# Attention queries and keys turned by VectorE squares and a round trip through device memory, in a two-layer hybrid decoder kernel

## The chip, the cores and the metric

The kernel runs on one core of a Trainium2 chip. The metric is the device time of one execution in microseconds (us). The kernel before takes 824.13 us, the median of three runs (824.0 to 824.54). One more execution was profiled; all rows of the trace come from it.

## What is computed (the reference, cut)

Two decoder layers on x of 256 tokens by 2048 columns, float32. Each layer reads four groups of heads off one projection h @ w_in (6232 columns), gates them, joins them and adds the product with w_out (2048 by 2048) to x.

```python
h = rmsnorm(x)
u = h @ w_in
y = concat(GLA(...) * silu(g_a), SSD(..., g_b), MLA(...) * silu(g_c), DIL(...) * silu(g_d))
x = x + y @ w_out

# MLA: 4 heads, q and k of 128 plain + 64 rotated columns, causal, 256 keys
q, k = rmsnorm(q) * q_head_g, rmsnorm(k) * k_head_g
q, k = rope on the last 64 columns
o = softmax(mask(q @ k.T * 192 ** -0.5)) @ v

# DIL: 4 heads of 128 columns, three dilated windows, rope on all columns
o = softmax(taps(q @ k.T * 128 ** -0.5)) @ v
```

To form q @ k.T on TensorE, queries and keys must lie with the 128 columns of a head on the partitions and the tokens along the row. They are produced the other way round, with tokens on the partitions. So each layer turns four matrices of 256 tokens by 512 columns: the plain parts of the MLA queries and keys, and the DIL queries and keys. That turning is what the change is about. The rotated MLA parts (a fifth such step, "mla rT") are turned as before.

## The kernel before, in words

**The weight stream.** Both layers are one long stream of weight units. A unit is two row blocks of 128 by up to 512 columns (512 KB for a unit of 1024 columns per partition, 278 KB in the narrow blocks). A layer has 144 numbered units n, 8 to a block of columns, and 4 extra ones for the MLA projections (STREAM, line 103), 148 in all. For each unit SP loads it into one of 4 buffers `raw` (line 495), ScalarE rounds it to `w_hi` (line 997), VectorE forms the rest `w_lo` (line 1354), and TensorE does 8 products with w_hi (lines 665 and 666) and then 4 with w_lo (line 674). w_hi and w_lo have 4 buffers each. So SP loads unit n only when VectorE has made w_lo of unit n - 4 (line 490), and ScalarE rounds unit n only when TensorE is through with unit n - 4 (line 996). In the text "lo 103" is the w_lo of unit 103, and "hi 95" the w_hi of unit 95.

**The side work.** All that is not this stream is cut into named steps, written between the units on each engine: after unit n of TensorE (PE_AT, line 186), after hi n on ScalarE (lines 1203 to 1297) and after lo n on VectorE (lines 1647 to 1768). Each engine works strictly in this order, so a step that waits holds up the hi or lo behind it. The dictionary ORDER (line 227) writes down the resulting order of the named steps; a step signals by a counter of its engine, and others wait for that count.

**The steps around the change**, in the numbers of the units they stand behind (TensorE / ScalarE / VectorE):

- VectorE 77 to 82 normalises the MLA heads, 83 and 84 do their rope, 86 and 87 normalise the DIL heads, 88 to 91 do their rope (lines 1578 to 1598).
- "mla qT", "mla kT", "mla rT" (lines 888 to 897, heads_T line 841): TensorE 85, 86, 87 turns 8 tiles of 128 by 128 each into PSUM, line 846; ScalarE copies them to SBUF behind 88, 89, 90 (line 1187).
- "dil qT", "dil kT" (lines 914 to 918): the same, TensorE 95 and 97, ScalarE 98 and 100.
- Scores "S 0" and "S 1" (line 849), two heads each: MLA at TensorE 89 and 93, DIL at 99 and 103. VectorE adds the mask and takes the row maximum three units later (smax, lines 1608 to 1616: 92, 96, 102, 106), ScalarE takes the exponential (line 1195, same units). For DIL, VectorE then multiplies by the tap counts (lines 1620 to 1626).
- "PT" turns the probabilities on TensorE (line 872; MLA 92 and 96, DIL 102 and 106), ScalarE copies them (line 1201; MLA 95 and 99). "O" multiplies by the values (lines 883 to 885; 94, 98, 104, 108), and VectorE scales the result (line 1644; 97, 101, 107, 111).
- The finished first and second groups are turned by VectorE itself, 16 transposes of 32 by 256 each (y_turn, line 1368; turn, line 1317), behind 97 to 100 and 101 to 104, into the first 1024 columns of u.
- ScalarE evacuates the gate blocks from PSUM (evac, line 1017) behind 90, 98, 106 and 114, with two table loads each (lines 1033 and 1036).

TensorE's side steps use two PSUM banks in turn; the step after next waits for the last reader of a bank (LAST_READER, line 196).

Of the kernel before, what the change touches and what calls it, by code (L numbers as in the profile page):

```python
# [27 lines left out]
ACT = mybir.ActivationFunctionType  # L28
# [158 lines left out]
for _n in range(8):  # L187
# [3 lines left out]
          "mla kv 1": KV_AT, "ssd Y": 76, "ssd yb": 81, "mla qT": 85, "mla kT": 86, "mla rT": 87, "mla S 0": 89, "mla PT 0": 92,  # L191
          "mla S 1": 93, "mla O 0": 94, "dil qT": 95, "mla PT 1": 96, "dil kT": 97, "mla O 1": 98, "dil S 0": 99,
# [7 lines left out]
               "mla cT": ("dve", "mla cT"), "mla qT": ("act", "mla qT"), "mla kT": ("act", "mla kT"), "mla rT": ("act", "mla rT"),  # L200
               "dil qT": ("act", "dil qT"), "dil kT": ("act", "dil kT")}
LAST_READER |= {f"gla level {n}": ("dve", f"gla merge {n}") for n in range(1, 8)}
LAST_READER |= {f"mla {w} {t}": ("act", f"mla {w} {t}") for w in ("q", "kv") for t in range(2)}
for _m in ("mla", "dil"):
    for _i in range(2):
# [25 lines left out]
        "mla cT, ssd Y, ssd yb, mla qT, mla kT, mla rT, "  # L231
        "mla S 0, mla PT 0, mla S 1, mla O 0, dil qT, mla PT 1, dil kT, mla O 1, dil S 0, dil PT 0, dil S 1, dil O 0, "
# [7 lines left out]
        "mla rT, mla P 0, ssd rs sum, mla PT 0, mla P 1, evac 11, dil qT, mla PT 1, dil kT, dil P 0, dil PT 0, "  # L240
# [7 lines left out]
        "mla n 0 0, mla n 0 1, ssd yT, mla n 1 0, mla n 1 1, mla rope products, mla rope, dil n 0 0, dil n 0 1, "  # L248
        "dil n 1 0, dil n 1 1, dil rope 0 products, dil rope 0, dil rope 1 products, dil rope 1, mla max 0, "
# [10 lines left out]
def build(nc, xT_d, x_d, pos_d, cols_d, w_d, params_d, gla_w2, gla_b,  # L260
          consts_d, masks_d, out_d):
    ctx = ExitStack()
    with ctx:
# [39 lines left out]
        eps, minus_half, log_scale = powers[:, 0:8], powers[:, 8:16], powers[:, 16:17]  # L303

# [65 lines left out]
        yturned = [u[:, t, 0:1024].rearrange("p (k s) -> p k s", k=4) for t in range(2)]  # L370
# [57 lines left out]
        warm = sem("warm")  # L428
        setup_chain = sem("setup_chain")
# [53 lines left out]
        @block.sync  # L483
        def _(sp):

            xT_load(sp, 0)
            sp.dma_start(raw[:, 0, 0:WB], weights(0, 0)[:, 0:WB]).then_inc(first_in, 16)
            for l in range(DEPTH):
                for g, n in enumerate(STREAM):
                    sp.wait_ge(split_done, l * PER_LAYER + g + 1)  # L490
                    if (l, n) == (0, 0):

                        sp.dma_start(raw[:, 0, WB:2 * WB], weights(l, n)[:, WB:2 * WB]).then_inc(weights_in[0], 16)
                    else:
                        sp.dma_start(raw[:, g % RAW, 0:unit_columns(n)], weights(l, n)).then_inc(weights_in[g % RAW], 16)
                    if (l, n) == (0, 0):
                        xT_load(sp, 1)
                    if l == 0 and n < len(XT_PARTS) - 2:
                        xT_load(sp, n + 2)
                    if (l, n) == (0, CONSTS_LOAD):  # L500
                        sp.dma_start(cst[:, 0:C_FR], consts_d[:, 0:C_FR]).then_inc(consts_in, 16)
                        sp.dma_start(lmask[:, :, :].rearrange("p a b -> p (a b)"), masks_d).then_inc(consts_in, 16)
                    if n in ROWS_LOAD:

                        i = ROWS_LOAD.index(n)
                        sp.wait_ge(row_out, 16 * (l + 1))
                        sp.dma_start(rows[:, 2 * i:2 * i + 2, :], row_d[2 * i:2 * i + 2, :].partition_broadcast(P)).then_inc(row_in[i], 16)
                    if n == PARAMS_LOAD[l]:
                        if l:

                            sp.wait_ge(*reached("dve", l - 1)(f"y {GB}"))
                        sp.dma_start(param_rows[:, :], params_d[l]).then_inc(params_in, 16)
                    if l == 0 and n in X_LOAD:
                        i = X_LOAD.index(n)
                        t, c = i // 2, slice(i % 2 * D // 2, (i % 2 + 1) * D // 2)
                        sp.dma_start(x[:, t, c], x_d.rearrange("o (t p) n -> p (o t) n", p=P)[:, t, c]).then_inc(x_in[i], 16)

            for i in range(len(OUT_PARTS)):
# [75 lines left out]
        def _(pe):  # L594
# [15 lines left out]
            for l in range(DEPTH):  # L610
# [277 lines left out]
                def mla_qT():  # L888
                    pe.wait_ge(*dve("mla rope"))
                    heads_T("mla qT", lambda t, h: mqk[:, t, h, 0:P])  # L890

                def mla_kT():
                    heads_T("mla kT", lambda t, h: mqk[:, t, 4 + h, 0:P])

                def mla_rT():
                    rr = mrr.rearrange("p t (a b) d -> p t a (b d)", b=2)
                    heads_T("mla rT", lambda t, h: rr[:, t, h])
# [3 lines left out]
                       "mla qT": mla_qT, "mla kT": mla_kT, "mla rT": mla_rT}  # L901

                def stages(n):
                    for name in PE_AT:
# [9 lines left out]
                        elif name == "dil qT":  # L914
                            pe.wait_ge(*dve("dil rope 1"))
                            heads_T(name, lambda t, h: dqk[:, t, h])
                        elif name == "dil kT":
                            heads_T(name, lambda t, h: dqk[:, t, 4 + h])
# [38 lines left out]
        def _(act_):  # L957
# [23 lines left out]
            for l in range(DEPTH):  # L981
# [202 lines left out]

                def heads_T(name, dst):
                    act_.wait_ge(*pe(name))
                    A_(dst, pair_of(name).rearrange("p b (k s) -> p (b k) s", k=2), ACT.Copy).then_inc(*signal("act", name))  # L1187
# [15 lines left out]
                for place, n in enumerate(STREAM):  # L1203
# [74 lines left out]
                    if n == slot("mla qT"):  # L1278
                        heads_T("mla qT", mqT)
                    if n == slot("mla kT"):  # L1280
                        heads_T("mla kT", mkT)
                    if n == slot("mla rT"):
                        heads_T("mla rT", mrT.rearrange("p a b s -> p (a b) s"))
                    if n == slot("dil qT"):
                        heads_T("dil qT", dqT)
                    if n == slot("dil kT"):
                        heads_T("dil kT", dkT)
# [14 lines left out]
        def _(v):  # L1302
# [29 lines left out]
            for l in range(DEPTH):  # L1332
# [314 lines left out]
                for place, n in enumerate(STREAM):  # L1647
# [157 lines left out]
```

## Time and profile before

| | us |
|---|---|
| median of 3 runs | 824.13 (824.0 to 824.54) |
| the profiled execution | 823.59 |
| its span, first to last instruction | 821.6 |
| TensorE busy in the span | 816.4 |
| VectorE busy | 625.2 |
| ScalarE busy | 478.2 |
| granted TensorE clock | 1.0 of full speed throughout |

The span is 2 us less than the execution's own time. Busy time is what the hardware recorded for each engine; idle time before an instruction is put down to what released it.

### The profile page before, as it was taken

The numbers are of one execution on the slowest core, as the hardware profiler recorded it, in microseconds if no ns is written. First come the engines' busy times: TensorE is split into PE (matmuls) and PEld (weight loads), VectorE is DVE, ScalarE is ACT, GpSimd is POOL, SyncE is SP. The second block draws the span as 40 slices with busy tenths as digits, with TensorE's granted clock in tenths as the row PEclk, the third lists the DMA queues.
The fourth block names the chain that finished last, engine by engine and source line by source line (L and its number), as shares of the span: only waits on it lengthen the run. The fifth ranks groups of instructions, "written<-read, shape, count | busy, mean of one in ns | idle before, by whom it ended". The sixth has DMA issues, their size and how long they took to land.

```text
span 821.6 us, 11397 instructions
## 1 busy us (share of the span) xinstructions
PE 816.4 (99%) x4244; PEld 693.0 (84%) x4244; DVE 625.2 (76%) x1118; ACT 478.2 (58%) x788; POOL 54.1 (7%) x64
## 2 busy tenths in 40 slices
PE   9999999999999999999999999999999999999998
PEld 5888888999888888888888888889998888888886
DVE  6678799876886986678965977979769868965542
ACT  6665534777865566433556464357697665654341
POOL 7200000200200000000000000002012000000000
PEclk9999999999999999999999999999999999999999
DMA  9956634566654445655576655457657433456653
GB/s 333 352 204 211 192 129 153 145 208 180 208 176 154 129 132 201 191 191 187 177 253 184 200 161 169 129 147 200 191 173 220 164 129 129 158 177 210 196 189 119
DMA packets 47607, 150.98 MB, mean 184 GB/s; under 512 B 5504, under 2 KB 6192, under 8 KB 47552
## 3 DMA queue, kind: packets, MB, share of 16 engines
q1 hardware_dynamic: 47040, 149.98, 57.0%
q8 instruction: 33, 0.54, 0.3%
q10 hardware_dynamic: 320, 0.21, 0.1%
q14 instruction: 22, 0.18, 0.1%
q0 software_dynamic: 192, 0.07, 0.1%
HBM read 148.13 MB, written 2.11 MB: 183 GB/s over the span
## 4 chain that ended last, share of the span: by engine, by line
PE 91%; DVE 7%; issue 2%; DMA 1%; SPq 0%; ACT 0%; DVEq 0%
PE gemm L665 26%; PE gemm L674 26%; PE gemm L666 26%; DVE arena L1323 3%; DVE w_lo L1354 2%; PE pairs L857 1%; PE pairs L846 1%; PE pairs L833 1%; PE pairs L838 1%; PE pairs L834 1%; PE pairs L795 1%; PE pairs L731 1%; DVE arena L1433 1%; PE pairs L872 1%; DMA u<-in_xT_dram 1%
## 5 line engine op out<-in xcount | busy, mean ns | idle before, releaser
L1354 DVE TENSOR_TENSOR w_lo<-raw,w_hi 128x1024 fp32r<-128x1024 f32 (+2 forms) x295 | 324.7, 1110 | 144.4 <-ACT w_hi L997 142.9
L665 PE MATMUL gemm<-w_hi,a_hi 128*128 128x512 f32 (+1 forms) x1144 | 421.6, 374 | 0.0
L666 PE MATMUL gemm<-w_hi,a_lo 128*128 128x512 f32 (+1 forms) x1144 | 414.4, 368 | 0.0
L997 ACT ACTIVATE w_hi<-raw 128x1024 fp32r<-128x1024 f32 (+2 forms) x295 | 281.0, 967 | 191.4 <-PE gemm L674 136.1
L674 PE MATMUL gemm<-w_lo,a_hi 128*128 128x512 f32 (+1 forms) x1144 | 281.8, 368 | 0.3
L665 PEld LDWEIGHTS gemm<-w_hi,a_hi 128*128 128x128 f32 x1144 | 215.2, 188 | 35.6 <-issue 1.3
L666 PEld LDWEIGHTS gemm<-w_hi,a_lo 128*128 128x128 f32 x1144 | 215.3, 188 | 33.0
L674 PEld LDWEIGHTS gemm<-w_lo,a_hi 128*128 128x128 f32 x1144 | 203.2, 188 | 36.6 <-DVE w_lo L1354 2.0
L573 POOL TENSOR_TENSOR st<-st,powers 128x4 f32<-128x4 f32 (+2 forms) x8 | 8.6, 1074 | 431.5 <-ACT arena L1075 213.4
L1195 ACT ACTIVATE arena<-arena,st 128x128 f32<-128x128 f32 (+1 forms) x32 | 13.1, 444 | 35.4 <-DVE st L1616 35.4
L1027 ACT ACTIVATE u<-gemm,st 128x512 f32<-128x512 f32 (+1 forms) x40 | 22.1, 605 | 18.8 <-PE gemm L674 18.8
L1323 DVE STREAM_TRANSPOSE arena<-u 32x256 f32<-32x256 f32 x64 | 27.9, 436 | 1.2
L1323 DVE STREAM_TRANSPOSE u<-o 32x256 f32<-32x256 f32 x64 | 27.9, 435 | 1.0
L1323 DVE STREAM_TRANSPOSE u<-x 32x256 f32<-32x256 f32 x48 | 20.9, 436 | 0.6
L1182 ACT ACTIVATE arena<-u 128x192 f32<-128x192 f32 (+1 forms) x64 | 20.6, 330 | 0.8 <-PE pairs L795 0.8
L1514 DVE SCALAR_TENSOR_TENSOR u<-arena,allp,u 128x256 f32<-128x256 f32 x48 | 20.9, 474 | 0.0
L1583 DVE SCALAR_TENSOR_TENSOR u<-u,sth,param_rows 128x192 f32<-128x192 f32 (+1 forms) x64 | 19.9, 378 | 0.0
L1058 ACT ACTIVATE arena<-arena 128x256 f32<-128x256 f32 x16 | 6.8, 424 | 18.0 <-DVE arena L1405 18.0
L1187 ACT ACTIVATE arena<-pairs 128x1024 f32<-128x1024 f32 x10 | 10.3, 1027 | 11.7 <-PE pairs L846 11.7
L731 PEld LDWEIGHTS pairs<-arena 128*128 128x128 f32 x112 | 14.7, 191 | 1.2
L1473 DVE COPY_PREDICATED o<-lmask,pairs 128x512 f32<-128x512 uint8 x14 | 12.4, 888 | 4.2 <-issue 4.2
L1314 DVE SCALAR_TENSOR_TENSOR a_lo<-u,allp,a_hi 128x256 fp32r<-128x256 f32 x28 | 14.3, 558 | 1.6 <-ACT a_hi L978 1.5
(200 smaller groups left out, 639.0 us busy)
## 6 DMA issues: line engine op xcount, KB each, us to landing
raw<-in_weights_dram SPq DMA_DIRECT2D x225, 512.0 KB, 4.1
raw<-in_weights_dram SPq DMA_DIRECT2D x64, 278.0 KB, 3.1
raw<-in_weights_dram SPq DMA_DIRECT2D x6, 384.0 KB, 3.4
x<-in_x_dram SPq DMA_DIRECT2D x4, 512.0 KB, 6.2
o<-ssd_rows SPq DMA_DIRECT2D x8, 256.0 KB, 4.9
param_rows<-in_params_dram SPq DMA_DIRECT2D x2, 904.0 KB, 7.1
u<-in_xT_dram SPq DMA_DIRECT2D x3, 512.0 KB, 8.1
out_dram<-x SPq DMA_DIRECT2D x3, 512.0 KB, 6.4
```

The lines of the kernel that those rows point to most:

```text
L665: pe.matmul(acc_t[t], a_hi[:, k, tok[t]], hi, start=k == 0, stop=False)
L666: pe.matmul(acc_t[t], a_lo[:, k, tok[t]], hi, start=False, stop=False)
L674: last = pe.matmul(acc_ps[:, b % 2, t, 0:w], a_hi[:, k, t * P:(t + 1) * P], lo, start=False, stop=k == KT - 1)
L731: last = pe.matmul(to, W[:, p, t * P:(t + 1) * P], Ql[n % 2][:, :, t, p, :], start=True, stop=True)
L997: A_(w_hi[:, g % SPLIT, 0:c], raw[:, g % RAW, 0:c], ACT.Copy).then_inc(hi_done, 1)
L1027: last = A_(u[:, t, c0 - N_GATE:c0 - N_GATE + w], acc_ps[:, b % 2, t, 0:w], ACT.Copy, scale=xrs[:, t:t + 1])
L1182: last = A_(sq[j % 8] if m == "mla" else sq[:, t, h, :], buf[:, t, 4 * i + h, :], ACT.Square, scale=buf.shape[-1] ** -0.5, accum_out=total ...
L1314: last = v.scalar_tensor_tensor(a_lo[:, k, :], part, gain(l, k), a_hi[:, k, :].bitcast(F32), ALU.mult, ALU.subtract)
L1323: last = v.transpose(to[32 * f:32 * f + 32, :, :, i, :], rows[32 * i:32 * i + 32, :, :, f, :])
L1354: TT(w_lo[:, g % SPLIT, 0:c], raw[:, g % RAW, 0:c], w_hi[:, g % SPLIT, 0:c].bitcast(F32), ALU.subtract).then_inc(split_done, 1)
L1514: last = STT(conv(f), xc[:, f, j:j + S], tap_weight(l, j, f), conv(f), ALU.mult, ALU.add)
L1583: last = STT(buf[:, t, 4 * i + h, :], buf[:, t, 4 * i + h, :], rs[:, j:j + 1], g, ALU.mult, ALU.mult)
```

## The change: what it does

The four turnings leave TensorE. Each becomes three steps.

1. VectorE transposes the 32 by 32 squares in place (turn_squares): two instructions of 128 partitions by 512 elements, one for each half of the tokens. They stand behind lo 79 (MLA queries), 83 (MLA keys), 90 (DIL queries) and 92 (DIL keys). The result goes to a new buffer `fold` or to columns 6656 to 7679 of the arena.
2. SP stores the 512 KB into device memory in one transfer, at unit at + 5, where `at` is the number above.
3. SP waits at unit at + 7 until that has landed, and loads it back in four transfers, one for each 32 partitions: 128 KB each, in pieces of 1 KB.

ScalarE then copies the result into the tiles that the scores read, behind hi 86, 88, 95 and 97 (before: 88, 89, 98, 100), from SBUF instead of PSUM. It waits for the four transfers of that name there. VectorE gets three new waits: the squares of the DIL queries and keys wait until the stores of the MLA ones have landed, and so does the first DIL rope (its scratch overlaps the MLA keys' squares). The turned y goes to the arena instead of u, and waits for "mla S 1" instead of "mla rT". SP's queue is the one that also loads the weights.

```diff
@@ PE_AT, LAST_READER and ORDER["pe"] @@
-          "mla kv 1": KV_AT, "ssd Y": 76, "ssd yb": 81, "mla qT": 85, "mla kT": 86, "mla rT": 87, "mla S 0": 89, "mla PT 0": 92,
-          "mla S 1": 93, "mla O 0": 94, "dil qT": 95, "mla PT 1": 96, "dil kT": 97, "mla O 1": 98, "dil S 0": 99,
+          "mla kv 1": KV_AT, "ssd Y": 76, "ssd yb": 81, "mla rT": 87, "mla S 0": 89, "mla PT 0": 92,
+          "mla S 1": 93, "mla O 0": 94, "mla PT 1": 96, "mla O 1": 98, "dil S 0": 99,
...
@@ ORDER["act"] @@
-        "mla rT, mla P 0, ssd rs sum, mla PT 0, mla P 1, evac 11, dil qT, mla PT 1, dil kT, dil P 0, dil PT 0, "
+        "mla rT, mla P 0, ssd rs sum, dil qT, mla PT 0, mla P 1, dil kT, evac 11, mla PT 1, dil P 0, dil PT 0, "
@@ ORDER["dve"] @@
-        "mla n 0 0, mla n 0 1, ssd yT, mla n 1 0, mla n 1 1, mla rope products, mla rope, dil n 0 0, dil n 0 1, "
-        "dil n 1 0, dil n 1 1, dil rope 0 products, dil rope 0, dil rope 1 products, dil rope 1, mla max 0, "
+        "mla n 0 0, mla n 0 1, ssd yT, mla q squares, mla n 1 0, mla n 1 1, mla k squares, mla rope products, mla rope, dil n 0 0, dil n 0 1, "
+        "dil n 1 0, dil n 1 1, dil rope 0 products, dil rope 0, dil q squares, dil rope 1 products, dil rope 1, dil k squares, mla max 0, "
@@ build @@
+        fold = sb("fold", [P, S * 4])
...
-        yturned = [u[:, t, 0:1024].rearrange("p (k s) -> p k s", k=4) for t in range(2)]
+        SQUARES = {}
+        SQUARES["mla q"] = fold[:, :], A(3072, 1024), 79
+        SQUARES["mla k"] = A(6656, 1024), u[:, 1, 0:1024], 83
+        SQUARES["dil q"] = fold[:, :], u[:, 0, 0:1024], 90
+        SQUARES["dil k"] = A(6656, 1024), u[:, 1, 0:1024], 92
+
+        HEADS_AT = {"mla q": 86, "mla k": 88, "dil q": 95, "dil k": 97}
+
+        yturned = [A(t * 1024, 1024, "p (k s) -> p k s", k=4) for t in range(2)]
...
+        squares_d = {name: nc.dram_tensor(name.replace(" ", "_") + "_squares", (P, 4 * S), F32, kind="Internal").ap() for name in SQUARES}
@@ SP @@
+            def squares_out(l, name):
+
+                sp.wait_ge(*reached("dve", l)(f"{name} squares"))
+                sp.dma_start(squares_d[name], SQUARES[name][0]).then_inc(squares_out_done[name], 16)
+
+            def squares_back(l, name):
+
+                sp.wait_ge(squares_out_done[name], 16 * (l + 1))
+                away, to = squares_d[name].rearrange("(i b) (f c) -> f b i c", b=32, f=4), SQUARES[name][1]
+                for f in range(4):
+                    sp.dma_start(to[32 * f:32 * f + 32].rearrange("b (i c) -> b i c", i=4), away[f]).then_inc(squares_in[name], 16)
...
+                    for name, (_, _, at) in SQUARES.items():
+                        if n == at + 5:
+                            squares_out(l, name)
+                        if n == at + 7:
+                            squares_back(l, name)
@@ TensorE @@
-                def mla_qT():
-                    pe.wait_ge(*dve("mla rope"))
-                    heads_T("mla qT", lambda t, h: mqk[:, t, h, 0:P])
-
-                def mla_kT():
-                    heads_T("mla kT", lambda t, h: mqk[:, t, 4 + h, 0:P])
-
                 def mla_rT():
+                    pe.wait_ge(*dve("mla rope"))
...
-                        elif name == "dil qT":
-                            pe.wait_ge(*dve("dil rope 1"))
-                            heads_T(name, lambda t, h: dqk[:, t, h])
-                        elif name == "dil kT":
-                            heads_T(name, lambda t, h: dqk[:, t, 4 + h])
@@ ScalarE @@
                 def heads_T(name, dst):
-                    act_.wait_ge(*pe(name))
-                    A_(dst, pair_of(name).rearrange("p b (k s) -> p (b k) s", k=2), ACT.Copy).then_inc(*signal("act", name))
+
+                    act_.wait_ge(squares_in[name], 16 * 4 * (l + 1))
+                    act_.wait_ge(*dve("mla rope" if name[:3] == "mla" else "dil rope 1"))
+                    A_(dst.rearrange("p h (t i a) -> p i (h t) a", t=T, i=4), SQUARES[name][1].rearrange("p (i c a) -> p i c a", i=4, a=32), ACT.Copy).then_inc(*signal("act", name + "T"))
...
+                    for name, to in (("mla q", mqT), ("mla k", mkT), ("dil q", dqT), ("dil k", dkT)):
+                        if n == HEADS_AT[name]:
+                            heads_T(name, to)
@@ VectorE @@
+            def turn_squares(to, rows):
+
+
+                to = to.rearrange("p (f k t a) -> p t k f a", f=4, k=4, t=T)
+                for t in range(T):
+                    last = v.transpose(to[:, t], rows[:, t].rearrange("p k (f b) -> p k f b", f=4))
+                return last
...
-                    v.wait_ge(*pe("mla rT"))
+
+                    v.wait_ge(*pe("mla S 1"))
...
+                def head_squares(name):
+
+                    m, i = name[:3], "qk".index(name[4])
+
+                    if m == "dil":
+                        v.wait_ge(squares_out_done["mla " + name[4]], 16 * (l + 1))
+                    elif l:
+                        v.wait_ge(squares_out_done["dil " + name[4]], 16 * l)
+                    v.wait_ge(*me(f"mla n {i} 1" if m == "mla" else f"dil rope {i}"))
+                    heads = (mqk if m == "mla" else dqk)[:, :, 4 * i:4 * i + 4, 0:P]
+                    turn_squares(SQUARES[name][0], heads).then_inc(*sig(f"{name} squares"))
...
                 def rope_products(name, after, x1, x2, tmp, nh, hd, step):
                     v.wait_ge(setup["act"], 1)
+                    if name == "dil rope 0":
+                        v.wait_ge(squares_out_done["mla k"], 16 * (l + 1))
...
+                    for name in HEADS_AT:
+                        if n == SQUARES[name][2]:
+                            head_squares(name)
```

## Rows read from the trace of the kernel before

**Rows 1.** The page, part 1: busy time, share of the span, instructions.
```profile
PE 816.4 (99%) x4244; PEld 693.0 (84%) x4244; DVE 625.2 (76%) x1118; ACT 478.2 (58%) x788; POOL 54.1 (7%) x64
```

**Rows 2.** The page, part 4: the chain that ended last, by engine.
```profile
PE 91%; DVE 7%; issue 2%; DMA 1%; SPq 0%; ACT 0%; DVEq 0%
```

**Rows 3.** The chain, first layer, then unit 103 of both: start, us, what.
```profile
232.63 0.87 PE pairs L846 x8
236.25 0.87 PE pairs L846 x8
...
242.60 0.91 PE gemm L674 x4
245.32 0.92 PE gemm L674 x4
...
296.26 0.92 PE gemm L674 x4
...
702.08 0.92 PE gemm L674 x4
```

**Rows 4.** Timeline of TensorE: PT of the first DIL heads, third part of unit 103.
```profile
293.61 0.82 PE L872 MATMUL pairs<-cst,arena 128*128 128x128 f32 x6
...
296.10 1.08 PE L674 MATMUL gemm<-w_lo,a_hi 128*128 128x512 f32 x4
```

**Rows 5.** Groups of instructions, shapes apart: count, busy us, mean ns, idle before.
```profile
L1323 DVE STREAM_TRANSPOSE u<-o 32x256 f32<-32x256 f32 x64 | 27.9, 435 | 1.0
L1419 DVE TENSOR_TENSOR arena<-o,arena 128x256 f32<-128x256 f32 x16 | 6.7, 420 | 0.6 <-ACT arena L1060 0.6
L1590 DVE TENSOR_TENSOR arena<-u,sincos 128x512 f32<-128x512 f32 x6 | 4.1, 684 | 0.0
L1187 ACT ACTIVATE arena<-pairs 128x1024 f32<-128x1024 f32 x10 | 10.3, 1027 | 11.7 <-PE pairs L846 11.7
```

**Rows 6.** Timeline of VectorE: lo 91, first and last of smax 0, lo 93, lo 97, y turn, lo 103.
```profile
245.03 1.22 DVE L1354 TENSOR_TENSOR w_lo<-raw,w_hi 128x1024 fp32r<-128x1024 f32 x1 [2.23 <-ACT w_hi L997]
...
248.52 0.29 DVE L1612 CUSTOM_DVE_ANT_0 arena<-pairs,cst 128x128 f32<-128x128 f32 x1
...
249.75 0.17 DVE L1616 TENSOR_SCALAR st<-st 128x4 f32<-128x4 f32 x1
252.80 1.23 DVE L1354 TENSOR_TENSOR w_lo<-raw,w_hi 128x1024 fp32r<-128x1024 f32 x1 [2.88 <-ACT w_hi L997]
...
266.74 1.22 DVE L1354 TENSOR_TENSOR w_lo<-raw,w_hi 128x1024 fp32r<-128x1024 f32 x1 [1.30 <-ACT w_hi L997]
...
290.92 1.78 DVE L1323 STREAM_TRANSPOSE u<-o 32x256 f32<-32x256 f32 x4
292.71 1.23 DVE L1354 TENSOR_TENSOR w_lo<-raw,w_hi 128x1024 fp32r<-128x1024 f32 x1
```

**Rows 7.** Timeline of VectorE, second layer: lo 103.
```profile
698.54 1.23 DVE L1354 TENSOR_TENSOR w_lo<-raw,w_hi 128x1024 fp32r<-128x1024 f32 x1
```

**Rows 8.** Timeline of ScalarE: hi 95, mla PT 0, hi 96, hi 97.
```profile
256.82 1.04 ACT L997 ACTIVATE w_hi<-raw 128x1024 fp32r<-128x1024 f32 x1
257.77 0.79 ACT L1201 ACTIVATE arena<-pairs 128x768 f32<-128x768 f32 x1
258.46 1.04 ACT L997 ACTIVATE w_hi<-raw 128x1024 fp32r<-128x1024 f32 x1
...
265.67 1.99 ACT L997 ACTIVATE w_hi<-raw 128x1024 fp32r<-128x1024 f32 x2
```

**Rows 9.** Transfers: issues, KB each, median us to landing; the first from 205 to 300 us.
```profile
raw<-in_weights_dram SPq DMA_DIRECT2D x28, 512.0 KB, 3.5
...
x<-in_x_dram SPq DMA_DIRECT2D x4, 512.0 KB, 6.2
o<-ssd_rows SPq DMA_DIRECT2D x8, 256.0 KB, 4.9
...
out_dram<-x SPq DMA_DIRECT2D x3, 512.0 KB, 6.4
```

More of the change, by code:

```diff
@@ L199 @@
                "ssd cum": ("dve", "ssd row"), "ssd gcol": ("act", "ssd gcol"), "ssd CB": ("dve", "ssd CB"), "ssd Y": ("dve", "ssd yT"), "ssd yb": ("act", "ssd y"),
-               "mla cT": ("dve", "mla cT"), "mla qT": ("act", "mla qT"), "mla kT": ("act", "mla kT"), "mla rT": ("act", "mla rT"),
-               "dil qT": ("act", "dil qT"), "dil kT": ("act", "dil kT")}
+               "mla cT": ("dve", "mla cT"), "mla rT": ("act", "mla rT")}
 LAST_READER |= {f"gla level {n}": ("dve", f"gla merge {n}") for n in range(1, 8)}
@@ L230 @@
         "gla level 6, gla level 7, gla out, ssd cum, ssd gcol, ssd CB, ssd xs, "
-        "mla cT, ssd Y, ssd yb, mla qT, mla kT, mla rT, "
-        "mla S 0, mla PT 0, mla S 1, mla O 0, dil qT, mla PT 1, dil kT, mla O 1, dil S 0, dil PT 0, dil S 1, dil O 0, "
+        "mla cT, ssd Y, ssd yb, mla rT, "
+        "mla S 0, mla PT 0, mla S 1, mla O 0, mla PT 1, mla O 1, dil S 0, dil PT 0, dil S 1, dil O 0, "
         "dil PT 1, dil O 1, yT 2, yT 3",
@@ L428, in build @@
         warm = sem("warm")
+        squares_out_done, squares_in = ({name: sem(name.replace(" ", "_") + end) for name in SQUARES} for end in ("_squares_out", "_squares_in"))
+        squares_d = {name: nc.dram_tensor(name.replace(" ", "_") + "_squares", (P, 4 * S), F32, kind="Internal").ap() for name in SQUARES}
         setup_chain = sem("setup_chain")
@@ L886, in values, with mla_rT @@
                     last.then_inc(*signal("pe", f"{m} O {i}"))
-                def mla_qT():
+                def mla_rT():
                     pe.wait_ge(*dve("mla rope"))
-                    heads_T("mla qT", lambda t, h: mqk[:, t, h, 0:P])
-                def mla_kT():
-                    heads_T("mla kT", lambda t, h: mqk[:, t, 4 + h, 0:P])
-                def mla_rT():
                     rr = mrr.rearrange("p t (a b) d -> p t a (b d)", b=2)
@@ L900, in _ @@
                        "gla out": gla_out, "ssd xs": ssd_xs, "ssd cum": ssd_cum, "ssd gcol": ssd_gcol, "ssd CB": ssd_CB, "ssd Y": ssd_Y, "ssd yb": ssd_yb, "mla cT": mla_cT,
-                       "mla qT": mla_qT, "mla kT": mla_kT, "mla rT": mla_rT}
+                       "mla rT": mla_rT}
                 def stages(n):
@@ L1183, in head_sums, with mla_rT @@
                     last.then_inc(*signal("act", f"{m} rs {i} sum"))
+                def mla_rT():
+                    act_.wait_ge(*pe("mla rT"))
+                    A_(mrT.rearrange("p a b s -> p (a b) s"), pair_of("mla rT").rearrange("p b (k s) -> p (b k) s", k=2), ACT.Copy).then_inc(*signal("act", "mla rT"))
                 def heads_T(name, dst):
-                    act_.wait_ge(*pe(name))
-                    A_(dst, pair_of(name).rearrange("p b (k s) -> p (b k) s", k=2), ACT.Copy).then_inc(*signal("act", name))
+                    act_.wait_ge(squares_in[name], 16 * 4 * (l + 1))
+                    act_.wait_ge(*dve("mla rope" if name[:3] == "mla" else "dil rope 1"))
+                    A_(dst.rearrange("p h (t i a) -> p i (h t) a", t=T, i=4), SQUARES[name][1].rearrange("p (i c a) -> p i c a", i=4, a=32), ACT.Copy).then_inc(*signal("act", name + "T"))
                 def probs(m, i):
@@ L1277, in _ @@
                         ssd_y()
[L1278 to L1281, printed above, removed]
+                    for name, to in (("mla q", mqT), ("mla k", mkT), ("dil q", dqT), ("dil k", dkT)):
+                        if n == HEADS_AT[name]:
+                            heads_T(name, to)
                     if n == slot("mla rT"):
[L1283 to L1287, printed above, removed]
+                        mla_rT()
                     for m in ("mla", "dil"):
```

## The prediction

> **What bounds the kernel now.** The page's busy line first: TensorE is busy 816.4 of 821.6 us, VectorE 625.2, ScalarE 478.2 [rows 1]. The chain that ended last says the same: 91% of it is TensorE [rows 2]. So work taken from TensorE pays one for one, as long as nothing else makes TensorE wait in its place. The chain in order of time gives the price of what is taken away: 8 transposes of 128 by 128 (line 846) are one block of 0.87 us, and from one such block to the next, with a weight unit between, are 3.62 us, where a unit alone takes 2.72 (from one set of four line 674 products to the next) [rows 3]. That is 0.90 us for each of the four groups, 3.6 us a layer, **7.2 us in all**: 0.9% of the time.
>
> Then the two engines that feed TensorE, around unit 103. VectorE has finished lo 103 at 292.71 + 1.23 = 293.94 us [rows 6], and TensorE begins the third part of unit 103, which reads it, at 296.10 [rows 4]: a margin of 2.15 us. The chain puts that part at 296.26 in the first layer and 702.08 in the second, and lo 103 of the second layer ends at 698.54 + 1.23 = 699.77 [rows 3, 7]; both layers have the same margin within 0.02 us. A second margin stands just before: the tap counts are done at 290.92, when the y turn begins, and the transposes of those probabilities start on TensorE at 293.61 [rows 4, 6], 2.7 us. Everything that VectorE does from lo 97 at 266.74 on, to lo 103, is one solid run, broken only by waits that are part of the same serial chain of scores. If lo 97 moves, lo 103 moves with it. So the question is where lo 97 lands.
>
> **What is removed.** 3.6 us of TensorE a layer, as above. From unit 97 on TensorE would be 3.6 us early and want lo 103 at 292.5. Since lo 103 now comes at 293.9, already an unmoved VectorE caps the gain at **2.15 us a layer**. What a layer gains is 2.15 minus X, X being the delay of lo 103.
>
> **What VectorE gets.** 16 square transposes, 8 a layer, of 128 by 512. No row shows that form. The nearest is the transpose of 32 by 256 at 435 ns; an add of 256 elements a row takes 420 and one of 512 takes 684 [rows 5]. The transposes cost as the adds do at 256, so I take 0.70 us at 512 and 1.42 for a pair (back to back transposes don't overlap: four of them take 1.78 [rows 6]). The lower end is 0.44 each, as if the row length didn't count, the upper 0.87, two of the small ones. In all 5.7 us a layer (3.5 to 7.0).
>
> What of it shows? The pair behind lo 79 lies in slack. The pairs of the MLA keys (83) and DIL queries (90), 2.8 us, eat the 2.23 us for which VectorE now idles before lo 91 [rows 6], and leave 0.5. The pair of the DIL keys (92) stands ahead of the mask and maximum of the first scores, whose last instruction ends at 249.9 [rows 6]: 0.5 + 1.42, so it ends 1.9 us later. ScalarE waits for just that (VectorE then idles 2.88 for the hi behind it [rows 6]), so hi 93 to hi 95 and lo 93 move by 1.9 as well.
>
> **What ScalarE gets.** The same eight copies of 128 by 1024, 1.03 us each from PSUM [rows 5]; the new ones read SBUF, and the w_hi copies of that size take 1.04 [rows 8]. No change in work. In place, there is one: the copy of the DIL queries now stands between hi 95 and "mla PT 0", where hi 95, PT 0 and hi 96 now follow each other without a gap from 256.82 to 259.5 [rows 8].
>
> **The transfers.** SP issues five more of them for each turning; its queue has no share in the chain [rows 2], and the weights it loads have four buffers, so issuing alone is covered. The store of 512 KB stands right behind a weight load. A load takes 3.5 us here; nearest stores of that size took 6.4, three in a row, and loads behind a weight load 6.2 at the crowded start [rows 9]. I take 5.0, with 3.5 and 7 as ends. Between store and wait lie two units, 5.4 us, so at 5.0 SP hardly stands, at 7 it stands 1.6 us with the weight loads behind it (a price only once their buffers run out). The way back is four issues behind a weight load, pieces of 1 KB. Nearest: 256 KB in such pieces, 4.9 us [rows 9]. I take 5.2 from the weight load before it to the last landing, 4 and 7 as ends.
>
> For the DIL queries: lo 93 ends at 254.03 + 1.9 = 255.9, the last quarter lands at 261.1. ScalarE has hi 95 at 257.9 + 1.9 = 259.8 [rows 8], waits 1.3 us, copies (0.95), does PT 0 (0.7) and hi 96 (0.95): hi 96 at 263.8 instead of 259.5. Then lo 96 (1.2), mask and maximum (1.4, from 248.52 to 249.92 for the first pair of heads), the exponentials and a hi behind them (2.9, the idle time before lo 93) [rows 6]: 269.3, less 0.2 for the overlap of instructions back to back, so 269.1. That stands against 265.67 + 1.04 = 266.7. **X = 2.4 us.** TensorE's own scores, 1.8 us early by then, no longer end that wait.
>
> The MLA keys are the tightest of the others: their loads back stand two units before ScalarE's copy, as the DIL queries' do, and behind that copy stand hi 89, the gate block and the rotated part, which "mla S 0" needs. By the same steps ScalarE stands there too, about 2 us, and the rotated part comes just in time; this is the slower rival's place. The new waits on VectorE are covered: between the store of the keys (behind lo 84) and the first DIL rope (behind lo 88) lie four units of VectorE's order, and between "mla S 1" and the y turn that now waits for it lies its whole maximum, ahead of lo 97.
>
> **The sum.** 2 x (2.15 - 2.4) = -0.5: the profiled 823.59 becomes 824.1. The profiled execution is 0.5 under the median of the three, so I predict **824.6**. TensorE would lose its 3.6 us a layer again as idle time, nearly all at the DIL probabilities and lo 103.
>
> **A rule against the change.** The rows price a 128 by 128 turning on TensorE at 0.87 / 8 = 0.11 us. The Trainium skill, VectorE: DVE Perf Modes, "Rules for kernel authors", says to use TensorE for a 128 by 128 transpose when PSUM will do as target; "The three transpose paths" there gives 390 ns for one on TensorE and 311 ns on VectorE, in squares. By its figure the 64 transposes would be worth 25 us, an estimate, not 7.2; the trace does not agree with the figure, since here they are pipelined. Its advice fits, as VectorE pays 5.7 us a layer for 3.6.
>
> **Rivals.**
> *Faster.* The squares or transfers are cheaper. If the DIL queries are back before hi 95, the 1.3 us wait goes and X is about 1.0; with 0.6 us a transpose instead of 0.7 about as much goes. Then 2 x 1.15 = 2.3 off, 822. At the cheap ends of both (X = 0.1) 4.1 off, 820. For it: the DIL queries' loads need to be only 1.3 us earlier; against: nothing gets X much under zero while VectorE has 5.7 us more to do. All 7.2 us (817) would need VectorE to be early, which no row offers. Chance 0.31.
> *Slower: the round trip is late.* One mechanism: store at 6 to 7 us, return at 6 to 7. SP then stands before the loads back, and ScalarE, in order, stands at the copies of the keys and DIL queries with the hi's behind it. In place: hi 89 and "mla S 0" (2 us), then lo 97. X becomes 4 to 6 and the layer loses 1.9 to 3.9 us: 828 to 832. It decides from about 0.4 us over my values on each leg. The dear transpose (0.87) alone gives X = 3.8, 827.4. For it: the stores' 6.4 us; against: those three stood in a row, ours come one at a time. Chance 0.33.
> *No change*, within 0.2% (1.65 us, about what a measurement of this kernel can tell from none): my forecast, X between 1.3 and 3.0. Chance 0.36. That the steps don't leave TensorE is excluded: the code that issues them is gone.
>
> **How the numbers follow.** 824.6 is the likeliest. The range takes in the faster case nearly to its cheap end and the late round trip to its middle: 820.5 to 829.5. Left out are a tenth on each side.
>
> **What would show it.** Line 846 with 16 products, not 80; 16 transposes near 0.70 us; TensorE idle before line 872 some 3 us a layer, released by the tap counts, and before line 674 by w_lo; ScalarE waiting over 1 us for the last quarter of the DIL queries; lo 103 2.4 us later against hi 80. Wrong, if TensorE shows less than 2 us of new idle time a layer, or if most of it stands at "mla S 0" and hi 89 instead.

## The result, and the profile after

The changed kernel takes 830.98 us, the median of five runs (829.52 to 833.96), against 824.13 before: a ratio of 1.0088 (95% interval 1.0069 to 1.0108). It is slower by 6.9 us, outside the predicted range. The profiled execution took 833.96 us, at the upper end of its runs; its span is 832.2 us, 10.6 more than before.

The page's busy line and the chain that ended last of the changed kernel, against [rows 1, 2]:

```profile
PE 814.2 (98%) x4180; PEld 688.7 (83%) x4180; DVE 633.9 (76%) x1134; ACT 477.5 (57%) x788; POOL 52.8 (6%) x64
...
PE 67%; DVE 16%; ACT 6%; DMA 5%; issue 5%; SPq 1%; DVEq 0%; ACTq 0%
```

The 64 products are gone. But TensorE holds only 67% of the chain, 91% before, and a transfer share of 5% is new. The groups of the new work (count, busy us, mean ns, idle before and what ended it), against [rows 5]:

```profile
L1213 ACT ACTIVATE arena<-u 128x1024 f32<-128x1024 f32 x6 | 6.3, 1056 | 20.6 <-DMA u<-mla_k_squares 16.3 <-DMA u<-dil_q_squares 4.3
L1352 DVE STREAM_TRANSPOSE fold<-u 128x512 f32<-128x512 f32 x8 | 5.2, 685 | 0.0
L1352 DVE STREAM_TRANSPOSE arena<-u 128x512 f32<-128x512 f32 x8 | 5.2, 684 | 0.0
```

A square transpose takes 0.685 us, the copy 1.06. ScalarE stood 16.3 us for the MLA keys and 4.3 for the DIL queries, over both layers (and 1.9 once for the MLA queries, in another group). What TensorE and SP's queue waited for in the changed kernel (us in total, times, longest):

```profile
PE pairs L903 <- DVE st L1668: 4.8, 2, 2.6
PE pairs L888 <- ACT arena L1207: 4.5, 2, 2.8
...
PE gemm L696 <- ACT w_hi L1017: 1.2, 1, 1.2
```

```profile
SPq L510 <- DMA mla_k_squares<-arena: 3.4, 2, 1.9
SPq L510 <- DMA dil_k_squares<-arena: 3.4, 2, 1.8
SPq L510 <- DMA mla_q_squares<-fold: 3.2, 2, 1.7
```

The first is the transposes of the DIL probabilities waiting for VectorE's tap counts, where it was expected. The second, "mla S 0" waiting for the rotated part on ScalarE, is nearly as large and was in no term of the forecast's sum. Its history stands in the chain, followed through 226 to 256 us of the first layer (start, us, what):

```profile
226.34 1.15 DVE w_lo L1383
227.50 0.35 SPq L521
227.85 0.04 issue
227.90 5.27 DMA mla_k_squares<-arena
233.18 0.33 SPq L510
...
234.51 7.72 DMA u<-mla_k_squares
242.25 0.02 ACT arena L1213
...
243.22 1.05 ACT w_hi L1017
```

The store stands behind the weight load that waits for lo 84 and lands at 233.2 us; the fourth quarter of the return takes 7.72 us and lands at 242.2. SP waited 1.9 us for the store's landing before it issued the return. Between the two it has to load units 89 and 90, which wait for lo 85 and lo 86, and VectorE makes these soon after lo 84, before the change too (its timeline before, lo 84, then lo 85 and 86):

```profile
223.17 1.22 DVE L1354 TENSOR_TENSOR w_lo<-raw,w_hi 128x1024 fp32r<-128x1024 f32 x1
...
225.51 2.35 DVE L1354 TENSOR_TENSOR w_lo<-raw,w_hi 128x1024 fp32r<-128x1024 f32 x2
```

The transfers issued from 227 to 237 us, weight loads among them, land late (count, KB each, median us), against [rows 9]:

```profile
raw<-in_weights_dram SPq DMA_DIRECT2D x4, 512.0 KB, 7.2
mla_k_squares<-arena SPq DMA_DIRECT2D x1, 512.0 KB, 5.3
u<-mla_k_squares SPq DMA_DIRECT2D x4, 128.0 KB, 4.5
```

And this is what stood behind that copy on ScalarE, in its timeline: hi 88, the keys, hi 89 and 90, the gate block with its two table loads, the rotated part.

```profile
231.96 1.07 ACT L1017 ACTIVATE w_hi<-raw 128x1024 fp32r<-128x1024 f32 x1 [0.97 <-DMA raw<-in_weights_dram]
242.25 1.06 ACT L1213 ACTIVATE arena<-u 128x1024 f32<-128x1024 f32 x1 [9.22 <-DMA u<-mla_k_squares]
243.22 1.99 ACT L1017 ACTIVATE w_hi<-raw 128x1024 fp32r<-128x1024 f32 x2
...
249.09 1.02 ACT L1207 ACTIVATE arena<-pairs 128x1024 f32<-128x1024 f32 x1
```

TensorE's timeline shows the three idle times that this and the later part cost in the first layer:

```profile
244.31 0.50 PE L696 MATMUL gemm<-w_hi,a_hi 128*128 128x512 f32 x1 [1.20 <-ACT w_hi L1017]
...
250.17 1.99 PE L888 MATMUL pairs<-arena 128*128 128x128 f32 x8 [2.83 <-ACT arena L1207]
...
299.80 0.87 PE L903 MATMUL pairs<-cst,arena 128*128 128x128 f32 x6 [2.18 <-DVE st L1668]
```

VectorE in the first layer: lo 96 now waits 3.65 us for a late hi, lo 97 starts at 275.74 (266.74 before) and lo 103 at 301.57 (292.71), one solid run again, against [rows 6]:

```profile
270.31 1.23 DVE L1383 TENSOR_TENSOR w_lo<-raw,w_hi 128x1024 fp32r<-128x1024 f32 x1 [3.65 <-ACT w_hi L1017]
...
275.74 1.23 DVE L1383 TENSOR_TENSOR w_lo<-raw,w_hi 128x1024 fp32r<-128x1024 f32 x1 [1.31 <-ACT w_hi L1017]
...
301.57 1.23 DVE L1383 TENSOR_TENSOR w_lo<-raw,w_hi 128x1024 fp32r<-128x1024 f32 x1
```

One more thing is new. The granted clock, 1.0 all through before, drops to its lower level behind two of these idle times, for 3.4 us each, and once more near the start, from 8.9 to 12.3 us, behind 1.5 us in which TensorE waited for a first w_hi. A table by stretches (us; PE, PEld, DVE, ACT, POOL busy; clock; DMA share; GB/s):

```profile
8.90:12.20 3.30, 3.30 (x9) 2.37 (x9) 2.97 (x6) 2.61 (x6) 2.94 (x5) 0.50 1.03 420
...
248.00:251.20 3.20, 1.03 (x7) 0.98 (x8) 3.20 (x6) 3.19 (x4) 0.00 (x0) 1.00 0.65 214
251.20:254.60 3.40, 3.40 (x14) 2.00 (x13) 3.40 (x5) 0.81 (x1) 0.00 (x0) 0.50 0.34 40
...
705.00:708.50 3.50, 0.92 (x6) 0.46 (x5) 1.88 (x12) 2.98 (x6) 0.00 (x0) 1.00 0.44 150
708.60:712.00 3.40, 3.40 (x13) 2.82 (x12) 3.30 (x7) 3.38 (x5) 0.00 (x0) 0.50 0.00 0
```

From 251.2 and from 708.6 us TensorE ran at 1.2 instead of 2.4 GHz, so 3.4 us did the work of 1.7. **The balance of the profiled execution:** TensorE's starts leave gaps of 7.2 us more than before in the first layer (1.36 at hi 89, 2.99 at mla S 0, 2.34 at the DIL probabilities, 0.48 at lo 103) and 5.4 in the second; less the 7.2 saved, that is 5.4; the two slow stretches add 3.3, and 1.4 were lost by 12 us into this execution (0.6 before the first slow stretch, the rest in it), 10.1 of the 10.6.

### The profile page after: what moved, and what is told of

Read it like the earlier page. It is cut to its first block, busy times and chain, and to the rows that moved or that the text cites. A ratio compares the mean times of both kernels' runs of the same rounds, so it can differ in the third digit from the quotient of the medians.

```text
span 832.2 us, 11337 instructions
## 1 busy us (share of the span) xinstructions
PE 814.2 (98%) x4180; PEld 688.7 (83%) x4180; DVE 633.9 (76%) x1134; ACT 477.5 (57%) x788; POOL 52.8 (6%) x64
## 4 chain that ended last, share of the span: by engine, by line
PE 67%; DVE 16%; ACT 6%; DMA 5%; issue 5%; SPq 1%; DVEq 0%; ACTq 0%
PE gemm L705 20%; PE gemm L696 20%; PE gemm L697 20%; DVE w_lo L1383 6%; DVE arena L1344 4%; ACT w_hi L1017 2%; DMA u<-mla_k_squares 2%; DMA mla_k_squares<-arena 1%; ACT arena L1221 1%; DMA u<-dil_q_squares 1%; DVE u L1613 1%; ACT arena L1202 1%; PE pairs L762 1%; DMA u<-in_xT_dram 1%; DVE arena L1463 1%
## 5 line engine op out<-in xcount | busy, mean ns | idle before, releaser
L1344 DVE STREAM_TRANSPOSE arena<-o 32x256 f32<-32x256 f32 x64 | 27.9, 436 | 1.0
L1213 ACT ACTIVATE arena<-u 128x1024 f32<-128x1024 f32 x6 | 6.3, 1056 | 20.6 <-DMA u<-mla_k_squares 16.3
L888 PE MATMUL pairs<-arena 128*128 128x128 f32 (+1 forms) x64 | 12.4, 337 | 4.5 <-ACT arena L1207 4.5
```

## The experiments

The median of before ran beside each; it was 823.9 to 824.2 us throughout. Two theories stood at first. **A:** the round trip lands late and holds ScalarE, which works in order. **B:** VectorE's extra 5.5 us a layer are the cost, wherever they stand.

### One half of the change alone

`e1_dil_only`: the MLA queries and keys stay on TensorE.

```diff
-          ... "ssd yb": 81, "mla rT": 87, ...
+          ... "ssd yb": 81, "mla qT": 85, "mla kT": 86, "mla rT": 87, ...
-        SQUARES["mla q"] = fold[:, :], A(3072, 1024), 79
-        SQUARES["mla k"] = A(6656, 1024), u[:, 1, 0:1024], 83
```

> Only the DIL queries and keys go the new way; the MLA ones are turned on TensorE as before. Theory A (the late round trip of the MLA keys holds ScalarE, and with it hi 89 and the first scores): that wait is gone, about 1.8 us a layer are saved, the DIL queries' wait stays: 822 to 825 us, no wait before mla S 0, no half clock behind it in the first layer. Theory B (VectorE's 5.5 us of squares a layer are the cost, wherever they stand): half of the loss stays, 827 to 828 us.

Measured: 826.77 us, ratio 1.0032 (1.0020 to 1.0044), outside the ranges of both theories and nearer to B's. The profiled execution (826.20 us) has no wait at mla S 0 and no slow stretch, but 2.6 us are lost where 3.6 should be gained. Three of the other four executions have a mean granted clock of 0.997 or 0.998, which points to slow stretches in this median too.

`e2_mla_only`: the other half.

```diff
-        SQUARES["dil q"] = fold[:, :], u[:, 0, 0:1024], 90
-        SQUARES["dil k"] = A(6656, 1024), u[:, 1, 0:1024], 92
+          ... "dil qT": 95, "mla PT 1": 96, "dil kT": 97, ...
```

> Only the MLA queries and keys go the new way; the DIL ones are turned on TensorE as before. Theory A: the loss at hi 89 and mla S 0 stays whole (2 to 4 us a layer against 1.8 saved), 827 to 830 us. Theory B: half of the loss, 827 to 828 us, but spread and not at mla S 0.

Measured: 826.54 us (twelve runs, 822.76 to 829.63), ratio 1.0027 (1.0012 to 1.0042), just under the ranges of both theories. ScalarE stood 13.2 us for the MLA keys, TensorE waited at mla S 0 in both layers. So A in its first form, the MLA keys alone, is too narrow: each half turns its 3.6 us of gain into a loss of about 2.5 (2.6 and 2.3), the MLA half before mla S 0, the DIL half before the DIL probabilities.

### The two costs apart

`e3_no_trip`: no transfers; ScalarE copies the squares where VectorE left them. The exchange between partitions is left out, VectorE's new waits for the stores go with the transfers, and the squares lie in other buffers.

```diff
-                        if n == at + 5:
-                            squares_out(l, name)
-                        if n == at + 7:
-                            squares_back(l, name)
...
-                    act_.wait_ge(squares_in[name], 16 * 4 * (l + 1))
+                    act_.wait_ge(*dve(name + " squares"))
```

> The transfers are left out (the squares stay on their partitions, ScalarE copies them as they are); VectorE's squares and ScalarE's copies stay where they are. Theory A: nothing waits for transfers; TensorE loses only what the squares cost, X about 1.0 a layer: 821 to 823 us. Theory B: as the changed kernel, 829 us or more.

Measured: 820.60 us, ratio 0.9955 (0.9943 to 0.9967): faster than before. What TensorE still waits for around the change is VectorE's serial run, once a layer at the tap counts and once at lo 103:

```profile
PE pairs L898 <- DVE st L1661: 2.1, 2, 1.1
...
PE gemm L700 <- DVE w_lo L1380: 0.7, 2, 0.3
```

`e4_small_squares`: the transfers stay; VectorE turns one eighth of the data, the rest is left out.

```diff
-                for t in range(T):
-                    last = v.transpose(to[:, t], rows[:, t].rearrange("p k (f b) -> p k f b", f=4))
-                return last
+                return v.transpose(to[:, 0, 0:1], rows[:, 0, 0:1].rearrange("p k (f b) -> p k f b", f=4))
```

> All transfers and waits stay; VectorE turns only 128 by 128 of each 128 by 1024 (one instruction of about 0.28 us instead of two of 0.685), the rest is left out. Theory A: the transfers come 1 to 2 us earlier but the MLA keys' wait on ScalarE stays: 825 to 829 us. Theory B: almost all of the loss goes, 819 to 821 us.

Measured: 826.72 us, ratio 1.0036 (1.0023 to 1.0049). If the 7.2 us of TensorE came whole, the time would be 824.0 - 7.2 = 816.8. The kernel without the trip is 3.8 above that, the one nearly without squares 9.9, both together (the changed kernel) 14.2. The two costs nearly add up (13.7 of 14.2), and the round trip is about 70%: 9.9 measured with almost no squares, 10.4 by what goes when the trip goes. The split is rough, since e4 keeps an eighth of the squares, and the changed kernel has slow stretches while the profiled execution of e4 has none. B falls as the main cause, but its 3.8 us are real.

### Where ScalarE waits

`e5_k_at_90`: the copy of the MLA keys stands behind the gate block.

```diff
-        "... ssd y, mla qT, mla kT, evac 10, "
+        "... ssd y, mla qT, evac 10, mla kT, "
-        HEADS_AT = {"mla q": 86, "mla k": 88, "dil q": 95, "dil k": 97}
+        HEADS_AT = {"mla q": 86, "mla k": 90, "dil q": 95, "dil k": 97}
```

> ScalarE copies the MLA keys behind hi 90 and the gate block instead of behind hi 88; nothing else moves. Theory A (ScalarE in order, held by the late MLA keys): hi 89, hi 90 and the gate block go ahead, the wait for the keys falls from 7 to 9 us to under 2, mla S 0 waits under 0.5 us, no half clock behind it: 2 to 4 us less than the changed kernel, 826 to 828 us. A rival, that the transfers slow the weight loads themselves: hi 89 and 90 stay late by their own loads and the time stays at 829 or more.

Measured: 827.39 us, ratio 1.0036 (1.0023 to 1.0050), as A had it. The wait for the MLA keys is gone from ScalarE, and so is TensorE's at mla S 0. What ScalarE still waits for are the DIL queries (and once, 1.8 us, the MLA queries); the second line is TensorE's largest wait:

```profile
L1213 ACT ACTIVATE arena<-u 128x1024 f32<-128x1024 f32 x6 | 6.3, 1058 | 5.4 <-DMA u<-dil_q_squares 5.4
...
PE pairs L903 <- DVE st L1668: 5.2, 2, 2.6
```

This is the kernel that the forecast described, without the keys' wait that its sum left out. TensorE idles 6.9 us around the change (5.2 at the DIL probabilities, 1.7 before the products with the values), against 7.2 forecast. Two slow stretches, from 293.5 and from 703.1 us, lie behind the waits at the DIL probabilities; at 1.7 us lost in each, 816.8 + 6.9 + 3.4 = 827.1.

`e6_dil_later`: the copies of the DIL queries and keys two units and one unit later.

```diff
-        "... ssd rs sum, dil qT, mla PT 0, mla P 1, dil kT, evac 11, mla PT 1, ..."
+        "... ssd rs sum, mla PT 0, mla P 1, dil qT, evac 11, dil kT, mla PT 1, ..."
-        HEADS_AT = {..., "dil q": 95, "dil k": 97}
+        HEADS_AT = {..., "dil q": 97, "dil k": 98}
```

> ScalarE copies the DIL queries behind hi 97 (was 95) and the keys behind hi 98 (was 97), so mla PT 0 and mla P 1 don't stand behind the queries' return. If that wait moves lo 97 as the prediction had it (1.3 us of its X), the wait before the first DIL probabilities on TensorE falls by 1.3 to 2.2 us a layer: 827 to 829 us. If VectorE's squares alone set lo 97: no change, 831.

Measured: 823.98 us (eleven runs, 821.92 to 827.68), ratio 1.0002 (0.9990 to 1.0014), 3 us better than the most that was expected. TensorE's wait for the tap counts fell from 4.8 to 1.0 us over both layers; the MLA keys' 16.0 us on ScalarE stayed.

`e9_copies_only`: both of these moves.

> The two moves of ScalarE's copies, with the DIL keys' squares left ahead of the first mask and maximum. If the place of those squares counts as the prediction had it (1.4 us of VectorE's chain in front of lo 97, against a cap of 2.15 us a layer): 819 to 821 us, with 1 to 1.5 us a layer at the DIL probabilities. If the copies alone did it: 817, as with all three.

Measured: 819.45 us, ratio 0.9945 (0.9933 to 0.9958). `e7_all_three` adds that the DIL keys' squares stand behind the first mask and maximum.

```diff
-        "... dil rope 1, dil k squares, mla max 0, "
-        "mla nmax 0, gated 1, ..."
+        "... dil rope 1, mla max 0, "
+        "mla nmax 0, dil k squares, gated 1, ..."
```

> Both moves of the copies, and the DIL keys' squares behind the first mask and maximum instead of ahead of them (into the 2.9 us for which VectorE waits before lo 93). Theory A and the prediction's X together: the waits at mla S 0 and the DIL probabilities nearly go, 817 to 821 us, under both kernels. If the transfers load the queue of the weights instead: 824 or more.

Measured: 817.16 us, ratio 0.9918 (0.9904 to 0.9931). **This beats both kernels**: 6.8 us under before, nearly all of the 7.2 that left TensorE. Over both layers ScalarE does not wait for the transfers at all, though SP's stores and returns stand where they did, and in the first layer the last quarter of the MLA keys still takes 9.0 us and lands at 242.1 us, as late as in the changed kernel (242.2):

```profile
L1213 ACT ACTIVATE arena<-u 128x1024 f32<-128x1024 f32 x6 | 6.3, 1058 | 0.0
```

The place of the DIL keys' squares alone is worth 819.45 - 817.16 = 2.3 us: VectorE had 2.88 us idle behind the maximum [rows 6], and none before it.

### When and how the transfers go

`e10_early`: the changed kernel, SP's two steps one unit earlier.

```diff
-                        if n == at + 5:
+                        if n == at + 4:
-                        if n == at + 7:
+                        if n == at + 6:
```

> The changed kernel with SP's store and its return each one unit earlier (at + 4 and at + 6). Theory A: the MLA keys and the DIL queries land about 2 us earlier, their waits on ScalarE fall by as much: 824 to 828 us. If it is the crowding of the transfers and not their late start: the landing moves by under 1 us and the time stays at 829 or more.

Measured: 820.93 us, ratio 0.9963 (0.9951 to 0.9976), 10 us under the changed kernel and 3 us below the range expected. ScalarE's wait for the MLA keys fell by 9.3 us, and those for both queries went:

```profile
L1213 ACT ACTIVATE arena<-u 128x1024 f32<-128x1024 f32 x6 | 6.3, 1050 | 7.0 <-DMA u<-mla_k_squares 7.0
```

One unit is 2.7 us on TensorE, and the waits fell by more than that. In the first layer the keys' store was issued 5.0 us earlier (222.94 us against 227.90), for between lo 83 and lo 84 VectorE has side work, the keys' squares among it. The store itself took longer, 6.5 us instead of 5.3, but the last quarter of the return took 4.4 instead of 7.7, and it landed 7.1 us earlier (235.15 against 242.23).

`e8_four_out_one_back`: the exchange between partitions is made by the store.

```diff
-                sp.dma_start(squares_d[name], SQUARES[name][0]).then_inc(squares_out_done[name], 16)
+                away = squares_d[name].rearrange("(f b) (i c) -> i b f c", b=32, i=4)
+                for i in range(4):
+                    sp.dma_start(away[i], SQUARES[name][0][32 * i:32 * i + 32].rearrange("b (f c) -> b f c", f=4)).then_inc(squares_out_done[name], 16)
...
-                for f in range(4):
-                    sp.dma_start(to[32 * f:32 * f + 32].rearrange("b (i c) -> b i c", i=4), away[f]).then_inc(squares_in[name], 16)
+                sp.dma_start(SQUARES[name][1], squares_d[name]).then_inc(squares_in[name], 16)
```

> Same data, same places; the store is made in four transfers of 32 partitions (1 KB pieces), the return in one of 128 partitions and 4 KB rows. If the narrow, fine-grained return is what comes late and delays the weight loads beside it: the return lands in about 4.5 us as one, but the stores take longer; the MLA keys' wait falls by 1 to 2 us a layer, 827 to 829 us. If the sum of two legs is what counts: 831, or worse as SP stands longer for the stores.

Measured: 826.69 us, ratio 1.0037 (1.0025 to 1.0050). The wait for the MLA keys fell from 16.3 to 10.4 us, 3 us a layer, more than expected, and TensorE no longer waits at mla S 0. In its transfers the four stores land as fast as the narrow loads did, and the return whole:

```profile
mla_k_squares<-arena SPq DMA_DIRECT2D x8, 128.0 KB, 3.7
u<-mla_k_squares SPq DMA_DIRECT2D x2, 512.0 KB, 4.9
```

`e11_one_back`: one store, one return of the data as stored (the exchange between partitions is left out).

```diff
-                for f in range(4):
-                    sp.dma_start(to[32 * f:32 * f + 32].rearrange("b (i c) -> b i c", i=4), away[f]).then_inc(squares_in[name], 16)
+                sp.dma_start(SQUARES[name][1], squares_d[name]).then_inc(squares_in[name], 16)
```

> The return is one transfer of 128 partitions and 4 KB rows of the data as stored (the exchange between partitions is left out); the store stays one transfer. If the narrow return in four costs by itself: it lands in about 4.4 us instead of 5 to 7.7 from the first issue on, neighbours' weight loads in under 5.5, 825 to 828 us, near the version with four stores and one return (826.7). If only the number of bytes and the two legs count: 831.

Measured: 825.75 us, ratio 1.0021 (1.0012 to 1.0030), as expected for a costly narrow return. A return in four, 32 partitions each, costs 4.3 us (by e8) to 5.2 us (by e11) against one of 128 partitions. How much of this is due to the four issues, 0.44 us each on SP, and how much to the narrow transfers, these runs don't part; the slow stretches behind the waits are in it too.

`e12_all_and_four_out` (e7 with e8) and `c2_all_and_early` (e7 with e10) ask whether the best version waits for anything more.

> All three moves together with the store in four and the return in one. With the waits gone the landing should no longer matter: 816.5 to 817.5 us, the same as with the three moves alone. If any wait for the return was left there, up to 0.5 us less.

Measured: 817.09 us, ratio 0.9918 (0.9905 to 0.9932).

> The three moves, and SP's store and return one unit earlier. Nothing waits for a transfer in the version with the three moves, so this changes nothing: 816.7 to 817.4 us. If a hidden wait was left, up to 0.5 us less.

Measured: 817.37 us, ratio 0.9920 (0.9906 to 0.9933). Neither differs from e7 beyond its interval, as expected: nothing waits there.

### The changed kernel again

> The changed kernel, unchanged. If waits alone make its time: 828 to 829 us, steady. If the half clock behind the waits adds to them: 829 to 834 again, scattered, with a half clock stretch of 3.4 us behind mla S 0 or the DIL probabilities in the profiled execution and about 1.7 us for each.

Measured: 831.62 us (four runs, 830.95 to 833.69), ratio 1.0097 (1.0083 to 1.0111). It repeats. Its profiled execution has two half clock stretches again, one behind mla S 0 of the second layer and one at the DIL probabilities of the first:

```profile
660.00:663.30 3.30, 3.30 (x13) 1.99 (x12) 3.30 (x5) 0.57 (x1) 0.00 (x0) 0.50 0.37 72
298.20:301.50 3.30, 3.14 (x11) 2.75 (x12) 3.18 (x8) 3.27 (x4) 0.00 (x0) 0.50 0.00 0
```

## Why the prediction was wrong

- **What bounds the kernel, and what is removed:** right. 7.2 us were predicted; the best version got 6.8 of them.
- **The price of a square transpose:** 0.70 us taken, 0.685 measured. ScalarE's copies: 1.04 and 1.06.
- **The cap of 2.15 us a layer and the serial run from lo 97 to lo 103:** the run moved as one piece (lo 97 by 9.0 us, lo 103 by 8.9), and TensorE's largest wait in total, 4.8 us, stands at the tap counts, as predicted; it is 4.5 at mla S 0. As a cap it holds only while VectorE is not early: in e7 lo 97 comes early and the layer gains more. "All 7.2 us would need VectorE to be early, which no row offers" was wrong: with mla S 1 1.8 us early and nothing in between, it is (lo 97 of e7 starts at 266.06 us, 266.74 before).
- **The squares' share of X:** about 1.0 us a layer without the transfers' waits was predicted (a gain of 2.3, 822); e3 gave 820.6, a gain of 3.6 against the 824.2 beside it. The squares hide a little better than worked out.
- **The step that failed** is the one on the MLA keys: "ScalarE stands there too, about 2 us, and the rotated part comes just in time". ScalarE stood 9.2 and 7.1 us, and TensorE then idled 3.0 and 1.8 us at mla S 0. Both legs were sized singly, 5.0 and 5.2 us. The store took 5.3 and 5.0, yet SP stood 1.9 and 1.6 us for it: the two units between store and wait were counted as 5.4 us, but VectorE finishes lo 84 and lo 86 only 3.5 us apart (224.4 and 227.9 us before, 227.5 and 230.9 after). The return was issued into three weight loads and took 9.1 us from its first issue to the last landing (233.18 to 242.2), in the second layer 7.0. The keys were called the tightest and named as the slower rival's place, with S 0 and hi 89 as its signs, and these are what the trace shows; but the sum was made with the DIL queries' term only, and the MLA keys' came in as nothing.
- **That step is not the whole of the miss.** Without that wait (e5) the kernel is 3.6 us faster; without the DIL queries' wait (e6), which the sum had in it, 7.0; without both (e9) 11.5 of the 14.2 us above the ideal are gone. What the two waits do together was not worked out either: hi 96 was predicted 4.3 us late and came 10.8 late (269.23 against 258.46), 1.4 of it from the start. X, forecast as 2.4, was thus 8.9 us by the clock of the trace, 7.4 without the start.
- **The slower rival** (chance 0.33) was right in place and size, 828 to 832 against 831, and that ScalarE stands in order with the hi's behind it. Of its two late legs, each set at 6 to 7 us, only the return was late (9.1 and 7.0 us); SP stood although the store took only 5.0 to 5.3.
- **The half clock** was in no part of the prediction. Behind the two waits it is 3.3 of the 10.6 us of the profiled execution, at some 1.7 us a stretch, and near the start up to 0.8 more. In e5 it roughly accounts for the distance between the forecast, 824.6, and the measured 827.4. The profiled execution was the slowest of the five and had the lowest mean clock (0.993; the others 0.995 to 0.998).
- **The rule of the Trainium skill** (VectorE: DVE Perf Modes, "Rules for kernel authors": TensorE for a 128 by 128 transpose when PSUM will do as target) would have kept the kernel as it was. For the change as made it was right, and for the version that beats both it was not: there 11 us of VectorE and 8 MB of transfers cost no more than 0.4 of the 7.2 us of TensorE saved, though TensorE does one such transpose in 0.11 us. The 390 ns that the prediction took from the same page stand there for bf16, and this kernel turns float32.

## What to carry to other kernels

When work leaves the bounding engine for a detour through others, look for the engine that works in order and must wait for the detour's end, and count what stands behind it: here the same detour, unchanged in work and bytes, cost 14.2 us, 2.7 once three waiting copies stood later, and 0.4 once a pair of squares stood later too. Starting the transfers one unit earlier brought most of it as well (10 us). A copy that waits for a transfer belongs behind everything that others need sooner; added work belongs behind an engine's serial dependency, where it idles, not ahead of it. And count the distance between two steps from the engine that paces them: two units of TensorE were 5.4 us, the same two on VectorE 3.5. A landing time read from a lone transfer is a lower end once five transfers and three loads go together.

## What the runs showed that was not expected

- **Narrow returns are slow.** By the records of single packets, those of 1 KB in the return of the MLA keys took 84 ns in the median and 144 at the ninetieth percentile (first layer), and 46 in e8, where the 1 KB pieces are in the store. Weight loads issued around that return landed after 6.4 to 8.3 us instead of 3.5. Whether the narrow pieces slow them is not shown: in e8 they took 4.2 to 5.4 us in the first layer, but in the second 4.6 to 6.1, where the changed kernel has 4.3 to 6.2. What within the memory path makes it so was not tried.
- **Clock.** Stretches of 3.4 us at half clock stand in 7 of the 15 profiled executions: the first of the changed kernel and its repeat, e2, e5, e6, e8 and e11. Each follows, or overlaps, an idle time of TensorE of 2.2 to 2.9 us around the change, except one each near 8.9 us in the first of the changed kernel and in e8, behind 1.5 and 1.3 us. Of the 18 idle times of 2.2 us or more in these executions, 10 had such a stretch; the 8 without are in e1, e4, e8, e11, the changed kernel and its repeat, up to 2.83 us long. e3, e7, e9, e10, e12 and c2 have no idle time of 2.2 us, no stretch, and a mean clock of 0.999 or 1.0 in every run. So such a wait may cost 1.7 us more than its own length. What decides stays open. It also scatters the times: in the twelve runs of e2 the three at a mean clock of 0.999 or 1.0 took 822.8 to 823.8 us, the nine at 0.996 to 0.998 took 825.7 to 829.6.
- **VectorE's transpose** of 32 by 32 squares in float32 costs as an add of the same row length does: 435 ns at 256 elements, 685 at 512.
